# Four edits to a two-layer diffusion step: the order of the start, and who builds the SSD weights

## The reference, cut to what matters

```
shift, scale, gate = split(silu(cond) @ w_mod[layer] + b_mod[layer], 3)
hm = rmsnorm(x, norm_g[layer]) * (1 + scale) + shift
```

```
y_diag = (decay * cb) @ (x * dt)      # decay = exp(cum[l] - cum[s]) where s <= l, else 0
cb[l, s] = C[l] . B[s]                # shared by the 4 heads of a group
y = y_f + flip(y_b) + d_skip * x      # forward scan, backward scan, skip
```

## Time and profile before

| what | us |
|---|---|
| median of three runs | 1192.13 |
| the profiled execution | 1192.75 |
| its span, first to last instruction | 1190.7 |
| TensorE busy, weight loads busy | 1118.3, 1045.6 |
| VectorE, ScalarE, GpSimd busy | 792.0, 445.0, 280.7 |

### The profile page before, as it was taken

How to read it: one execution, slowest core, us unless ns; L and a number is a source line. 1 busy time by engine, 2 the same in 40 slices (tenths; PEclk the granted TensorE clock), 3 DMA queues, 4 the chain that set the end, 5 groups by cost and what they waited for, 6 DMA issues and landing times. The chain is left out here.

```text
span 1190.7 us, 19216 instructions
## 1 busy us (share of the span) xinstructions
PE 1118.3 (94%) x7195; PEld 1045.6 (88%) x7195; DVE 792.0 (67%) x1388; ACT 445.0 (37%) x848; POOL 280.7 (24%) x423
## 2 busy tenths in 40 slices
PE   5999999999999999999889899999989898979997
PEld 3799999999999988889889898998989898857785
DVE  2654434757575444566698988979797979776454
ACT  5322212121212133354444545454445353544321
POOL 1200000000000000021044444353444535364001
PEclk9899999999999999999999999999999999989999
DMA  9743222354543252305342433433343433272702
GB/s 326 247 133 106 67 74 89 116 172 133 164 141 107 71 198 86 83 18 179 102 124 68 142 89 103 132 102 111 107 128 103 128 89 111 78 263 80 293 21 89
DMA packets 177879, 148.05 MB, mean 124 GB/s; under 512 B 7004, under 2 KB 156868, under 8 KB 177428
## 3 DMA queue, kind: packets, MB, share of 16 engines
q1 hardware_dynamic: 172772, 130.08, 35.4%
q0 software_dynamic: 4608, 16.83, 4.3%
q10 hardware_dynamic: 432, 0.21, 0.1%
HBM read 134.32 MB, written 12.78 MB: 124 GB/s over the span
## 5 line engine op out<-in xcount | busy, mean ns | idle before, releaser
L264 DVE TENSOR_TENSOR w_lo<-raw_w,w_hi 128x1024 fp32r<-128x1024 f32 x128 | 157.9, 1235 | 86.4 <-ACT w_hi L258 84.9
L258 ACT ACTIVATE w_hi<-raw_w 128x1024 fp32r<-128x1024 f32 x128 | 134.7, 1054 | 114.6 <-PE PS L291 72.1
L291 PE MATMUL PS<-h_hi,w_hi 128*128 128x320 f32 x720 | 164.7, 310 | 0.0
L291 PE MATMUL PS<-h_lo,w_hi 128*128 128x320 f32 x720 | 164.1, 309 | 0.0
L291 PE MATMUL PS<-h_hi,w_lo 128*128 128x320 f32 x720 | 164.0, 309 | 0.0
L1350 PE MATMUL PS<-h_hi,w_hi 128*128 128x320 f32 x480 | 118.7, 329 | 10.6 <-DVE big L1539 10.6
L291 PEld LDWEIGHTS PS<-h_hi,w_hi 128*128 128x128 f32 x720 | 120.1, 188 | 3.4 <-ACT big L946 2.5
L291 PEld LDWEIGHTS PS<-h_hi,w_lo 128*128 128x128 f32 x720 | 120.5, 188 | 0.0
L291 PEld LDWEIGHTS PS<-h_lo,w_hi 128*128 128x128 f32 x720 | 120.3, 188 | 0.0
L1350 PE MATMUL PS<-h_lo,w_hi 128*128 128x320 f32 x480 | 111.6, 314 | 0.0
L1350 PE MATMUL PS<-h_hi,w_lo 128*128 128x320 f32 x480 | 111.3, 314 | 0.0
(11 more groups left out here) (229 smaller groups left out, 2304.5 us busy)
## 6 DMA issues: line engine op xcount, KB each, us to landing
raw_w<-in_fc_w_in_dram SPq DMA_DIRECT2D x48, 512.0 KB, 4.3
raw_w<-in_ssd_w_in_dram SPq DMA_DIRECT2D x48, 512.0 KB, 5.1
big<-l_scr SPq DMA_DIRECT2D x40, 512.0 KB, 4.4
big<-in_w_mod_dram POOLq DMA_DIRECT2D x16, 1024.0 KB, 5.4
big<-in_w_mod_dram SPq DMA_DIRECT2D x16, 512.0 KB, 7.9
raw_w<-in_fc_w_out_dram SPq DMA_DIRECT2D x16, 512.0 KB, 3.6
raw_w<-in_ssd_w_out_dram SPq DMA_DIRECT2D x16, 512.0 KB, 8.0
y_scr<-big SPq DMA_DIRECT2D x40, 128.0 KB, 1.8
```

Of the source, the lines that this page charges most:

```text
L258: act.activation(w_hi[:, slot, :], raw_w[:, slot, :], ACT.Copy).then_inc(hi_ready, 1)
L264: dve.tensor_tensor(w_lo[:, slot, :], raw_w[:, slot, :], w_hi[:, slot, :].bitcast(F32), ALU.subtract).then_inc(lo_ready, 1)
L291: mm = pe.matmul(PS[:, 2 * pair + s, 0:HALF], w[:, slot, ws], h[:, kt, s * HALF:(s + 1) * HALF], start=(kt == 0 and n == 0), stop=(kt == K ...
```

## The change

It has four parts.

1. ScalarE's first activation is now a Silu of one column (`cond_first`), and the Silu of `cond` stands behind the third Square in `norm_act`. VectorE pads `cond` behind the third normalised tile.
2. `wm_used` counts halves: slices 0 to 3 of the columns 1 are loaded when the first half of the first modulation product is done, slices 4 to 7 when the second is.
3. `split_lo` of unit 1 stands behind the second slice of h, inside `h_dve`.
4. The weights inside a chunk: ScalarE copies `cb` out of PSUM (cbc) and builds `upper * (dt_f - dt_b) + dt_b` (dtm, four activations a chunk), and VectorE multiplies by `cb` in one instruction. What is missing on the diagonal is `cb * dt_b` of that token, so a new step cbd takes the diagonal of `cb` and adds `cb * dt_b` to the skip factor `dx`. cbm, W and the four instructions of G are gone, and SC0 and several steps of the lists are moved. The last group's lists have the same new steps.

```diff
+                if t == 2:
+                    act.wait_ge(cond_landed, 32)
+                    act.activation(cond[:, :, :], cond[:, :, :], ACT.Silu).then_inc(cond_ready, 1)
...
             for k in range(4 * c, 4 * c + 4):
+                if k == 2:
+                    split_lo(dve, 1, 1)
...
-            mm.then_inc(wm_used, 1)
+                mm.then_inc(wm_used, 1)
...
-                dve.tensor_copy(all_tables(DTO, 8), by_group(tDT))
+                dtv = tDT.rearrange("p c (g d h) -> p c g d h", g=G, d=2)
+                for c in range(NT):
+                    dve.tensor_tensor(all_tables(DTO, 4)[:, c], dtv[:, c, :, 0], dtv[:, c, :, 1], ALU.subtract)
+                    dve.tensor_copy(all_tables(DTO + 4, 4)[:, c], dtv[:, c, :, 1])
...
             "PE": """
-                P00 CB0 P01 T0 P02 T1 T2 P03 T3 T4 P04 P05 P06 CB1 H0 S0 P07 P10 P11 P12 P13 P14 P15 P16 P17 S1 P20 S2 SC0 P21 P22
+                P00 CB0 P01 T0 P02 T1 T2 P03 T3 T4 P04 P05 P06 CB1 H0 S0 P07 P10 P11 P12 P13 P14 P15 P16 P17 S1 P20 S2 P21 P22 SC0
                 P23 P24 Y0 Y1 P25 P26 P27 P30 P31 P32 P33 P34 P35 YT0 P36 P37 Y2 Z00 Z01 YT1 Z10 Y3 Z11 Z20 Z21 YT2 Z30 Y4 Z31 Z40
...
             "ACT": """
-                tok0 tok1 tok2 exp0 tok3 tok4 exp1 hev0 hi0 cen0 exp2 tanh0 exp3 hi1 cen1 scev0 tanh1 exp4 hi2 cen2 sq0 yn0 ytev0
+                dtm0 tok0 cbc0 tok1 tok2 exp0 dtm1 tok3 tok4 exp1 hev0 cbc1 cen0 hi0 dtm2 tanh0 exp2 cen1 hi1 dtm3 scev0 exp3 tanh1 dtm4
+                exp4 hi2 cen2 sq0 yn0 ytev0
...
             "DVE": """
-                M0 cbm0 M1 G0 cbm1 G1 M2 hup0 tap0 M3 fin0 lo0 hup1 lo1 tap1 hup2 fin1 G2 yt0 M4 G3 ya0 lo2 yt1 tap2 ya1 fin2 tap3
+                M0 M1 G0 G1 cbd0 tap0 hup0 M2 fin0 lo0 hup1 M3 hup2 lo1 tap1 fin1 G2 yt0 M4 G3 ya0 lo2 yt1 tap2 ya1 fin2 tap3
...
             "Pool": """
-                W0 xw0 W1 grp0 hd0 W2 xw1 W3 hd1 xw2 xw3 hd2 W4 u0 rs0 u1 rs1 u2 rs2 u3 u4 rs3 rs4
+                xw0 grp0 hd0 xw1 hd1 xw2 xw3 hd2 u0 rs0 u1 rs1 u2 rs2 u3 u4 rs3 rs4
...
                     elif k == 1:
-                        pe.wait_ge(cbm_done, 2 * g + 2)
+                        pe.wait_ge(cbc_done, 2 * g + 2)
...
+                elif ev == "cbc":
+                    act.wait_ge(cb_ready, 2 * g + k + 1)
+                    src, dst = (PS[:, 7, :].rearrange("p (c l) -> p c l", c=4), cb[:, 0:4, :]) if k == 0 else (PS[:, 5, 0:P], cb[:, 4, :])
+                    act.activation(dst, src, ACT.Copy).then_inc(cbc_done, 1)
+                elif ev == "dtm":
+                    r = (B.par + k) % 2
+                    tab = table(gt[:, B.par, :], DTO, 8)
+                    if k >= 2:
+                        act.wait_ge(g_done, b0 + k - 1)
+                    for h in range(4):
+                        e = act.activation(wt[:, r, h, :], upper, ACT.Identity, bias=tab[:, k, 4 + h:5 + h], scale=tab[:, k, h:h + 1])
+                    e.then_inc(dtm_done, 1)
...
+                elif ev == "cbd":
+                    dve.wait_ge(cbc_done, 2 * g + 2)
+                    dve.tensor_tensor(cbj, cb, ident.unsqueeze(1).to_broadcast([P, NT, P]), ALU.mult).then_inc(cbj_done, 1)
+                    dve.wait_ge(cbj_done, g + 1)
+                    dve.tensor_reduce(cbd, cbj, mybir.AxisListType.X, ALU.add).then_inc(cbd_done, 1)
+                    dve.wait_ge(cbd_done, g + 1)
+                    dve.tensor_tensor(dx, cbd.unsqueeze(2).to_broadcast([P, NT, 4]), table(tab, DTO + 4, 4), ALU.mult).then_inc(dx_step, 1)
+                    dve.wait_ge(dx_step, g + 1)
+                    dve.tensor_tensor(dx, dx, tab[:, 200:204].unsqueeze(1).to_broadcast([P, NT, 4]), ALU.add).then_inc(dx_done, 1)
                 elif ev == "G":
-                    dve.wait_ge(w_done, b0 + k + 1)
-                    for h in range(4):
-                        e = dve.scalar_tensor_tensor(out=wt[:, r, h, :], in0=cbm[:, 0, k, :], scalar=table(tab, DTO, 4)[:, k, h:h + 1],
-                                                     in1=wt[:, r, h, :], op0=ALU.mult, op1=ALU.add)
-                    e.then_inc(w_full, 1)
+                    dve.wait_ge(dtm_done, b0 + k + 1)
+                    dve.wait_ge(cbc_done, 2 * g + (1 if k < 4 else 2))
+                    dve.tensor_tensor(wt[:, r, :, :], wt[:, r, :, :], cb[:, k, :].unsqueeze(1).to_broadcast([P, 4, P]), ALU.mult).then_inc(w_full, 1)
...
-                    xd = pool.tensor_tensor(hv(uu[:, r, :]), xh(k), heads(gt[:, B.par, 200:204]), ALU.mult)
+                    if k == 0:
+                        pool.wait_ge(dx_done, g + 1)
+                    xd = pool.tensor_tensor(hv(uu[:, r, :]), xh(k), heads(dx[:, k, :]), ALU.mult)
...
             def chunk_load(c):
                 for t in range(KT):
+                    if c == 1 and t % 4 == 0:
+                        sp.wait_ge(wm_used, t // 4 + 1)
...
-            sp.wait_ge(wm_used, 1)
             chunk_load(1)
             first_load(3)
-            sp.wait_ge(wm_used, 2)
+            sp.wait_ge(wm_used, 4)
...
+            act.wait_ge(ones_ready, 1)
+            act.activation(cond_first, ones[:, 0:1], ACT.Silu)
             norm_act(act)
-            act.wait_ge(cond_landed, 32)
-            act.activation(cond[:, :, :], cond[:, :, :], ACT.Silu).then_inc(cond_ready, 1)
```

More of the change, by code:

```diff
@@ L129, in build_step @@
         condp = carve(21504, KT, 32)
+        cond_first = carve(21504 + 256, 1)
         xn = carve(5120 + 8192, 2, D)
@@ L177, in build_step @@
         lfb = take(2, 8, P)
-        cbm = take(2, NT, P)
+        cb = take(NT, P)
+        cbj = take(NT, P)
         ea = take(2, 4, P)
@@ L181, in build_step @@
         wt = take(2, 4, P)
-        take(1024)
+        cbd = take(8)[:, 0:NT]
+        dx = take(NT, 4)
+        take(1024 - 28)
         xws = take(4, 512)
@@ L239, in build_step @@
             "proj_free", "z_ready", "zth_done", "cen_done", "tap_step", "th_done", "conv_done", "grp_done"))
-        (tr_ready, tok_done, h0_landed, h_T, hs0_done, cb_ready, cbm_done, xw_done, st_ready, st_done, hd_done) = (sem(n) for n in (
-            "tr_ready", "tok_done", "h0_landed", "h_T", "hs0_done", "cb_ready", "cbm_done", "xw_done", "st_ready", "st_done", "hd_done"))
+        (tr_ready, tok_done, h0_landed, h_T, hs0_done, cb_ready, cbc_done, xw_done, st_ready, st_done, hd_done) = (sem(n) for n in (
+            "tr_ready", "tok_done", "h0_landed", "h_T", "hs0_done", "cb_ready", "cbc_done", "xw_done", "st_ready", "st_done", "hd_done"))
         (sc_ready, sc_done, small_stored, m_done, exp_done, g_done, y_ready, t_done, pool_step, u_done, a_step, gz_done) = (sem(n) for n in (
@@ L1277, in build_step @@
             "ACT": """
-                tok0 tok1 tok2 tok3 tok4 hev0 exp0 exp1 eh0 eh1 eh2 eh3 scev0 eh4 eh5 exp2 sq0 eh6 eh7 yn0 ytev0 exp3 sq1 yn1 ytev1
-                exp4 sq2 yn2 ytev2 sq3 sq4 yn3 yn4 ytev3 ytev4
+                tok0 tok1 tok2 tok3 tok4 hev0 cbc0 cbc1 dtm0 exp0 dtm1 exp1 eh0 eh1 eh2 eh3 scev0 eh4 eh5 dtm2 exp2 sq0 eh6 eh7 yn0 ytev0 dtm3 exp3 sq1 yn1 ytev1
+                dtm4 exp4 sq2 yn2 ytev2 sq3 sq4 yn3 yn4 ytev3 ytev4
                 """.split(),
             "DVE": """
-                M0 cbm0 hup0 cbm1 M1 hup1 el0 el1 hup2 G0 el2 M2 yt0 el3 G1 ya0 G2 M3 yt1 el4 el5 G3 ya1 yt2 el6 el7 M4 ya2 G4 yt3
+                M0 hup0 M1 hup1 el0 el1 hup2 cbd0 G0 el2 M2 yt0 el3 G1 ya0 G2 M3 yt1 el4 el5 G3 ya1 yt2 el6 el7 M4 ya2 G4 yt3
                 ya3 ya4
@@ L1285, in build_step @@
             "Pool": """
-                xw0 hd0 xw1 hd1 xw2 hd2 xw3 W0 W1 W2 u0 W3 rs0 W4 u1 rs1 u2 rs2 u3 u4 rs3 rs4
+                xw0 hd0 xw1 hd1 xw2 hd2 xw3 u0 rs0 u1 rs1 u2 rs2 u3 u4 rs3 rs4
                 """.split(),
@@ L1564, in ssd_dve @@
                     e.then_inc(m_done, 1)
[L1565 to L1570, removed]
-                elif ev == "G":
-                    dve.wait_ge(w_done, b0 + k + 1)
-                    for h in range(4):
-                        e = dve.scalar_tensor_tensor(out=wt[:, r, h, :], in0=cbm[:, 0, k, :], scalar=table(tab, DTO, 4)[:, k, h:h + 1],
-                                                     in1=wt[:, r, h, :], op0=ALU.mult, op1=ALU.add)
-                    e.then_inc(w_full, 1)
+                elif ev == "cbd":
[7 more added lines that the diff above has]
+                    dve.tensor_tensor(dx, dx, tab[:, 200:204].unsqueeze(1).to_broadcast([P, NT, 4]), ALU.add).then_inc(dx_done, 1)
+                elif ev == "G":
+                    dve.wait_ge(dtm_done, b0 + k + 1)
+                    dve.wait_ge(cbc_done, 2 * g + (1 if k < 4 else 2))
+                    dve.tensor_tensor(wt[:, r, :, :], wt[:, r, :, :], cb[:, k, :].unsqueeze(1).to_broadcast([P, 4, P]), ALU.mult).then_inc(w_full, 1)
                     dve.wait_ge(w_full, b0 + k + 1)
@@ L1626, in ssd_pool @@
                     e.then_inc(xw_done, 1)
-                elif ev == "W":
-                    pool.wait_ge(cbm_done, 2 * g + (1 if k < 4 else 2))
-                    if k >= 2:
```

(8 more changed lines are left out.)

8 lines of the change are left out of this document (3 added, 5 removed).

## The result

The changed kernel takes 1179.16 us (median of 4 runs, 1177.56 to 1182.1) against 1192.93 of the kernel before on the same chip. The ratio is 0.9887, 95% interval 0.9875 to 0.9899: 13.8 us faster, where I had predicted 33.6. It lies outside my range (1149 to 1173). The profiled execution took 1177.56 us, with a span of 1175.8.

A forecast was written before the change was run, and what follows sets the result against it. TensorE, busy 94%, could gain only its waits and lower-clock time: 29.4 + 5.8 - 6.0 + 3.8 - 0.6 + 1.2 = 33.6 us off 1192.75 gives 1159.2 (1158.5 on the median's scale); 8-in-10 range 1149 to 1173.

The forecast's parts named there:

- The waits: Seven SSD bodies: TensorE's waits of P20 for tap0 and SC0 for hup1 both go, gaining 29.4 us.
- The clock: Four stretches behind those waits in the bodies: TensorE no longer drops to 1.2 GHz, gaining 5.8 us.
- ScalarE's side: Each body: dtm ahead of tok0 and tok3 delays T2 and S0, 0.85 us a body, 6.0 us lost in all.
- The step that failed: Bodies, behind SC0: the next late step would be hup2, at 681 against Y0 at 683.3.
- VectorE stays the late one somewhere behind Y0: Rival, bodies: half of the 35 us comes back as a TensorE wait behind Y0, giving 1176; chance 0.06.
- The last group: Last group: shorter G1 and G3 bring ya0 and the YT steps earlier, gaining 3.8 us, bounds 0 and 9.
- Tables: Tables: one copy becomes five subtractions and five copies, ahead of an sz TensorE waits for; 0.6 us lost.
- The start: Start: table load, lo of unit 1 and reload by halves together gain 1.2 us, bounds 0 and 2.5.
- the second cover: Start: the modulation row's copy stands behind unit 0's hi, which waits for its DMA, so gains at most 0.55 us.
- The signs that I had named for "wrong": Bodies: SC0 or Y0 waiting for VectorE, L1399 waiting over 0.5 us for GpSimd's xw, or periods above 61 us.
- the five products: Bodies, VectorE: G0's and G1's four products and cbd0's could each wait 0.6 us for GpSimd, eating tap0's slack.

The follow-up runs named there:

- yt0_order: Kernel after with two moves in the bodies: ScalarE's exp4 behind sq0, VectorE's ya0 ahead of G3; 1172.87 us.
- yt0_act_only: Kernel after with one move in the bodies, ScalarE's exp4 behind sq0, VectorE's list unchanged; 1174.99 us.
- tok_first: Kernel after with ScalarE's tok copies put ahead of the dtm steps (tok0 to tok2 before dtm0, tok3 and tok4 before dtm1); 1189.75 us.
- t_spread_last: Kernel after with T2 to T4 and S0 later on TensorE, body lists reordered; last group: M2 behind G1, eh0 to eh3 ahead of dtm1; 1162.44 us.

## Why the prediction was wrong

By its own terms, for the profiled execution (forecast 1159.2, measured 1177.56):

- **The waits, 29.4 us: right.** By the start times in the kernel before, P20's wait costs 1.8 and SC0's 2.7 us, 4.5 a body against my 4.2; both are gone. tap0 was forecast for 670.2 and came at 670.08, hup1 for 677.5 and came at 677.98, SC0 for 680.5 and came at 679.65. That tap0 came so close is luck in part: the product of cbd0 started 0.9 us sooner than the 668.2 I had, and the step took 2.8 us in place of 2.0.
- **The clock, 5.8 us: right.** The granted clock of 594 to 1010 us rises from 0.98 to 1.00. Before, three of the six distances between bodies are 64.1 to 64.2 us and three 62.4 to 62.6; after, all six are 61.0 to 61.4.
- **ScalarE's side, -6.0 us: right in kind, too small.** dtm is 0.49 us an instruction, 1.64 for four (I took 1.55). T2's wait shows as 0.46 us in its row but takes 0.67 between starts (1.25 us for T1 and T2 in place of 0.58), H0 and S0 take 0.58 more: 1.25 a body, 8.8 us in all.
- **The step that failed.** "Next late would be hup2 for Y0: [...] against Y0 at 683.3." I followed the chain of late things to Y0 and stopped there. The next late one was yn0 for YT0, 1.85 us a body between starts, 13 us in all. I had this as the rival "VectorE stays the late one somewhere behind Y0, and half of the 35 us comes back as a wait there: 1176", gave it 0.06, and wrote against it that TensorE waits there nowhere now. That was the mistake: no wait is not slack. YT0 had 0.36 us of it when I was about to bring TensorE there 4 us sooner. The mechanism was that rival's, and so was the time, within 2 us; the time is so close in part because other terms missed as well. yt0_order, yt0_act_only and tok_first show the wait moving with the branch in both directions.
- **The last group, 3.8: measured 1.2.** I counted G's shorter work and not M2's wait for its DMA ahead of yt0; t_spread_last, which moves M2 and eh0 to eh3, gets 4.9 us out of this group.
- **Tables, -0.6: measured -0.5.** Right.
- **The start, 1.2: nothing, or a small loss.** I bounded it at 0 from below, without a reason that excludes a loss. I had the second cover (hi0 waiting for unit 0) but not the first, the landing of slices 4 to 7, nor GpSimd's longer lo part beside the moved lo of unit 1. The copy of the modulation row came at 25.38 us and not at my 24.8. How much of it is the clock stays open: the first layer-0 matmul starts between 61.9 and 65.6 us in the ten traces with the new start, and between 62.0 and 63.4 in the four with the old one.

Together: 13 + 2.8 + 2.6 + 1.7 for the start = 20.1 us missed, less 2.1 for P20 and SC0, which cost 4.5 and not 4.2 a body: 18.0 of the 18.4 us.

The signs that I had named for "wrong" did their work: the period is 61.3, above 61. No wait of SC0 or Y0 for VectorE appeared. S0's wait was 0.4 us in the mean and 0.6 at its longest, where I had named 0.5.

The Trainium skill (SBUF — State Buffer, Who interferes with whom) says that a VectorE instruction with two SBUF inputs blocks against GpSimd's SBUF reads. The trace agrees. Of the five products for which I had allowed 3 us, the four of G0 and G1 take 0.69 to 0.73 us. The product of cbd0 takes 1.23 us at 667.26, beside GpSimd's hd0 (667.05 to 668.96), and 0.81 in the last group, where GpSimd is idle:

```profile
1039.64 0.81 DVE L1593 TENSOR_TENSOR big<-big,cst 128x640 f32<-128x640 f32 x1
```

The same shows where I had not looked: M4's four instructions take 2.53 us at 688.17, beside u0, against 1.14 for four with GpSimd idle, in the last group (1047.57, shown above). That is 1.4 us in the branch, ahead of ya0, where YT0 waits 1.7. The kernel before had it too (2.94 us at 690.48), and no run takes it away, so what it costs in time is not shown.
